# Attention values with the value matrix held in the array, two heads in column halves, and the exponentials scaled on ScalarE first

## What is computed

```python
def attend(q, k, v):
    s = jnp.einsum('bqhgd,bkhd->bhgqk', qblk, k) * scale
    p = jax.nn.softmax(s, axis=-1)
    return jnp.einsum('bhgqk,bkhe->bqhge', p, v)
...
    o1 = attend(dq[:, :, :, 0, None, :], dk[:, :, :, 0, :], dv)
    o2 = attend(dq[:, :, :, 1, None, :], dk[:, :, :, 1, :], dv)
    od = (o1 - lam * o2)[:, :, :, 0, :]
    od = rmsnorm(od, subln_g) * (1.0 - lambda_init)
    og = attend(gq.reshape(B, S, GQA_KV_HEADS, GQA_GROUP, HEAD_DIM), gk, gv)
    o = jnp.concatenate([od.reshape(B, S, DIFF_WIDTH), og.reshape(B, S, GQA_WIDTH)], axis=-1)
    return o @ w_out
```

## Time and profile before

| | |
|---|---|
| Time, median of 3 runs | 1468.42 us (1465.95 to 1468.68) |
| Profiled execution, its own time | 1464.05 us |
| Its span | 1462.2 us |
| Mean granted TensorE clock | 0.968 of full speed |
| Busy: PE, DVE, ACT, POOL | 1323.5, 1109.0, 630.1, 317.5 us |
| The 16 units | from 128.96 us (first exponential) to about 205 us |

### The profile page before, as it was taken

The page is one execution under the profiler, slowest core; times in us unless marked ns, Lnnn a source line. Parts: engine busy times, 40 slices in busy tenths (PEclk is TensorE's granted clock), DMA queues, the critical chain, the costliest instruction groups (busy, mean ns, idle before and its releaser), DMA issues.

```text
span 1462.2 us, 16524 instructions
## 1 busy us (share of the span) xinstructions
PE 1323.5 (91%) x5512; PEld 874.0 (60%) x5512; DVE 1109.0 (76%) x2315; ACT 630.1 (43%) x1322; POOL 317.5 (22%) x307
## 2 busy tenths in 40 slices
PE   9998899998797978697887799999999999999998
PEld 3876664543353424253343346678888877788887
DVE  6688857876776776766667777869998577799974
ACT  5343733222221222222221225567776445677752
POOL 0000003544344444344434430000110000011100
PEclk9999999999898989899898899999999999999999
DMA  9624457999999999999999996434545434345540
GB/s 392 271 116 190 162 248 317 419 422 421 421 422 420 421 422 421 421 414 421 414 421 407 414 416 265 171 117 157 189 173 196 156 118 167 115 178 198 201 144 30
DMA packets 50437, 416.32 MB, mean 285 GB/s; under 512 B 5552, under 2 KB 5680, under 8 KB 7088
## 3 DMA queue, kind: packets, MB, share of 16 engines
q0 software_dynamic: 36864, 268.45, 44.4%
q1 hardware_dynamic: 13488, 146.82, 26.3%
HBM read 414.20 MB, written 1.05 MB: 284 GB/s over the span
## 4 chain that ended last, share of the span: by engine, by line
PE 39%; DVE 36%; DMA 13%; issue 6%; ACT 3%; POOL 2%; DVEq 0%; SPq 0%; POOLq 0%; ACTq 0%
PE ps L1199 9%; DVE arena_r L592 8%; DMA ring<-in_uv,ids 6%; DMA arena<-in_uv,ids 6%; PE ps L1278 4%; PE ps L1280 4%; PE ps L1279 4%; DVE arena L2519 4%; DVE ring L2237 4%; DVE arena L2237 2%; DVE arena L2511 2%; DVE arena L2521 2%; PE ps L1172 2%; PE ps L1018 2%; PE ps L907 2%
## 5 line engine op out<-in xcount | busy, mean ns | idle before, releaser
L1199 PE MATMUL ps<-ring,arena 128*128 128x512 f32 x632 | 294.3, 616 | 51.5 <-ACT arena L1714 51.5
L2237 DVE CUSTOM_DVE_ANT_0 ring<-ring,arena 128x1024 f32<-128x1024 f32 x158 | 190.6, 1225 | 85.9 <-DMA ring<-in_uv,ids 85.5
L1199 PEld LDWEIGHTS ps<-ring,arena 128*128 128x128 f32 x632 | 122.3, 197 | 213.5 <-issue 143.6
L1486 PE MATMUL ps<-hpair,arena_r 128*128 128x512 f32 x704 | 244.3, 394 | 0.0
L592 DVE TENSOR_TENSOR arena_r<-ring,arena_r 128x1024 fp32r<-128x1024 f32 x152 | 185.5, 1223 | 57.3 <-ACT arena_r L577 53.6
L1199 PE MATMUL ps<-arena 128*128 128x512 f32 x392 | 186.5, 622 | 46.5 <-ACT arena L1714 46.3
L793 POOL DMA_INDIRECT ring<-in_uv,ids x158 | 177.8, 1126 | 227.2 <-PE ps L1199 175.4
L1488 PE MATMUL ps<-hpair,arena_r 128*128 128x256 f32 x704 | 195.0, 277 | 0.0
L577 ACT ACTIVATE arena_r<-ring 128x1024 fp32r<-128x1024 f32 x152 | 158.8, 1053 | 59.0 <-PE ps L1280 58.1
L793 POOL DMA_INDIRECT arena<-in_uv,ids x98 | 104.3, 1064 | 352.2 <-issue 246.5
L1199 PEld LDWEIGHTS ps<-arena 128*128 128x128 f32 x392 | 76.9, 199 | 148.5 <-issue 92.0
(11 more groups left out here) (337 smaller groups left out, 2049.2 us busy)
## 6 DMA issues: line engine op xcount, KB each, us to landing
ring<-in_lw SPq DMA_DIRECT2D x39, 2048.0 KB, 7.8
ring<-in_b1w SPq DMA_DIRECT2D x14, 2048.0 KB, 8.8
ring<-in_b1w SPq DMA_DIRECT2D x9, 1024.0 KB, 16.7
ring<-in_lw SPq DMA_DIRECT2D x8, 1024.0 KB, 5.1
wqb<-in_wq SPq DMA_DIRECT2D x4, 1024.0 KB, 9.0
arena<-in_wq SPq DMA_DIRECT2D x3, 1024.0 KB, 13.4
ring<-in_uv,ids POOLq DMA_INDIRECT x158, 16.9
ring<-in_lw SPq DMA_DIRECT2D x2, 1088.0 KB, 10.2
```

Of the source, the lines that this page charges most:

```text
L1199: last = nc.tensor.matmul(ps[:, 4 + 2 * c + b, :], diag[:, k % 4, :], vrows[place(n, k)][:, b * 512:(b + 1) * 512], start=False, stop=(clo ...
L1486: nc.tensor.matmul(ps[:, bank, :].rearrange("p (t n) -> p t n", t=2), high_of(l, p)[:, cols_], hpair[:, :, k, :], start=(k == 0), stop=Fal ...
L2237: V.tensor_tensor_reduce(out=urows[at], in0=urows[at], in1=hrow[:, c, :], scale=1.0, scalar=0.0, op0=ALU.mult, op1=ALU.add, accum_out=dots ...
```

## The change

Units of the grouped kind are done the other way round. The values of one key/value head (128 keys by 64 columns) become the weights and the transposed probabilities (128 keys by 128 queries) the moving side. The result comes out transposed: head dimension on partitions 0 to 63 for the first head, 64 to 127 for the second, 128 queries in the free dimension. The two heads so use two column halves of the array, and the loop over key chunks is now the outer one. This result is what `out_sums` needs as weights, so it is copied straight into the grouped half of `orow` (`grouped_rows`) and used from there: `turned` and `heads_in` for the grouped blocks go away, for both chunks.

Since queries are no longer on partitions, the reciprocals of the sums can't be applied on the way out. A new step, `act_scale`, scales the two exponentials of a grouped unit in place on ACT, before they are transposed; it waits for the reciprocals of DVE (`rz_ready`), and PE's `turn` waits for it (`scaled`). On ACT the order within a turn of the loop becomes: exponentials of m, `act_pt(m - 1)`, `act_rows(m - 2)`, `act_scale(m)`. `values(m)` waits until the rows of unit m - 1 are out of bank 6, where it was unit m - 2.

```diff
+        def of_kind(m):
+            kind = [(t < DIFF) for c, t in units()]
+            return sum(k == kind[m] for k in kind[:m + 1])
+        def grouped_rows(c):
+            return orow[:, c, 512:1024].rearrange("p (k n) -> p k n", k=4)
+        def act_scale(act, m):
+            act.wait_ge(rz_ready, of_kind(m))
+            for s in range(2):
+                last = nc.scalar.activation(E[:, m % 2, s, :], E[:, m % 2, s, :], ACT.Copy, scale=rz4[:, m % 4, s:s + 1])
+            last.then_inc(scaled, 1)
...
             else:
-                for s in range(2):
-                    last = nc.scalar.activation(orow[:, c, t * P + s * HD:t * P + (s + 1) * HD],
-                                                src[:, s * HD:(s + 1) * HD], ACT.Copy, scale=rz4[:, m % 4, s:s + 1])
+                last = nc.scalar.activation(grouped_rows(c)[:, t - DIFF, :], src, ACT.Copy)
...
-                pe.wait_ge(probs_ready, m + 1)
+                pe.wait_ge(probs_ready if t < DIFF else scaled, of_kind(m))
...
-                if m >= 2:
-                    pe.wait_ge(pv_out, m - 1)
+                if m >= 1:
+                    pe.wait_ge(pv_out, m)
...
-                    for s in range(2):
-                        for kc in range(4):
-                            last = nc.tensor.matmul(ps[:, 6, at + s * HD:at + (s + 1) * HD],
+                    for kc in range(4):
+                        for s in range(2):
+                            last = nc.tensor.matmul(ps[s * HD:(s + 1) * HD, 6, at:at + P],
+                                                    vrow[:, kc, 512 + s * HD:512 + (s + 1) * HD],
                                                     PT[:, m % 2, s, kc * P:(kc + 1) * P],
-                                                    vrow[:, kc, 512 + s * HD:512 + (s + 1) * HD],
-                                                    start=(kc == 0), stop=(kc == 3))
+                                                    start=(kc == 0), stop=(kc == 3), skip_group_check=True)
...
+                c = 1 if bank in (2, 3) else 0
                 for i in steps:
                     k = OUT_ORDER[i]
-                    last = nc.tensor.matmul(ps[:, bank, :], oT[:, k, :], out_weight(n, k), start=(i == 0),
+                    heads = oT[:, k, :] if k < DIFF else grouped_rows(c)[:, k - DIFF, :]
+                    last = nc.tensor.matmul(ps[:, bank, :], heads, out_weight(n, k), start=(i == 0),
...
                 if m == 10:
                     pe.wait_ge(pv_out, 8)
-                    pe.wait_ge(mod_out, MOD_A + 5)
-                    turned(0, range(4, KD), 7)
                 elif m == 11:
                     pe.wait_ge(rows_ready, 2)
-                    pe.wait_ge(o_out, 1)
+                    pe.wait_ge(mod_out, MOD_A + 5)
                     turned(0, range(4), 7)
...
-            turned(1, range(4, KD), 4)
             pe.wait_ge(exp_done, 32)
-            pe.wait_ge(o_out, 3)
             out_sums(0, 2, 0, 1)
...
+                if m >= 1:
+                    act_pt(act, m - 1)
                 if m >= 2:
                     act_rows(act, m - 2)
-                if m >= 1:
-                    act_pt(act, m - 1)
+                if t >= DIFF:
+                    act_scale(act, m)
...
-                elif m == 11:
-                    heads_in(1, range(4, KD), 7)
                 elif m == 12:
-                    heads_in(2, range(4), 7, con("subg"))
+                    heads_in(1, range(4), 7, con("subg"))
...
-            heads_in(3, range(4, KD), 4)
...
-                    dve.sem_inc(probs_ready, 1)
+                    dve.sem_inc(rz_ready, 1)
```

More of the change, by code:

```diff
@@ L359, in program @@
         pt_done, pt_act, pv_done, pv_out = (sem(n) for n in ("pt_done", "pt_act", "pv_done", "pv_out"))
+        rz_ready, scaled = sem("rz_ready"), sem("scaled")
         gd_ready, gb_done, gb_out = sem("gd_ready"), sem("gb_done"), sem("gb_out")
@@ L1041, in _ @@
                     pe.wait_ge(pv_out, 8)
-                    pe.wait_ge(mod_out, MOD_A + 5)
-                    turned(0, range(4, KD), 7)
                 elif m == 11:
                     pe.wait_ge(rows_ready, 2)
-                    pe.wait_ge(o_out, 1)
+                    pe.wait_ge(mod_out, MOD_A + 5)
                     turned(0, range(4), 7)
                 elif m == 12:
-                    pe.wait_ge(o_out, 2)
+                    pe.wait_ge(o_out, 1)
                     out_sums(0, 7, 0, 1)
@@ L1147, in _ @@
             cleared(4, 5)
-            pe.wait_ge(o_out, 4)
+            pe.wait_ge(o_out, 2)
             out_sums(0, 2, 4, 5, 6, 7)
@@ L1687, in _ @@
             rows_in(0, (0, 7))
-            heads_in(4, range(4), 0, con("subg"))
+            heads_in(2, range(4), 0, con("subg"))
             softmax(0, 0)
@@ L2073, in attn_probs @@
                         .then_inc(probs_ready, 1)
-                    dve.wait_ge(probs_ready, m + 1)
+                    dve.wait_ge(probs_ready, of_kind(m))
                 else:
-                    dve.sem_inc(probs_ready, 1)
+                    dve.sem_inc(rz_ready, 1)
             attn_max(0)
```

## The result

Seven executions of the changed kernel have a median of 1471.5 us (1470.1 to 1473.7), seven of the kernel before on the same chip 1466.6 us (1465.3 to 1468.7). The ratio is 1.0028 with a 95% interval of 1.0019 to 1.0038: some 4.1 us slower by the ratio, 4.9 us by the medians. The profiled execution took 1470.54 us (span 1468.7). The forecast of 1470.1 stood on a median before of 1468.4; measured side by side the kernel before is 1.8 us faster than that, so the forecast's own statement, 1.7 us slower, is too small by 2.4 to 3.2 us although its absolute time is near.

What follows compares the result with a forecast made beforehand. No engine alone bounds the units; PE's chain ends them and passes delay on unchanged. ACT's scales delay turn(11) by 3.0 us, shorter PE work leaves +1.7: 1468.4 + 1.7 = 1470.1 us, range 1465.5 to 1474.0.

Steps and rivals of the forecast that it cites:

- The likeliest case: Units 7 to 11: ACT is the longest and delays PE's end of the units, +1.7 us; chance 0.42.
- The rival on the other side: Units: scales hide in ACT's idle time, only PE's gain shows, -3 to -4.4 us, 1464.5; chance 0.12.
- The values: Grouped values on PE: 16 matmuls in column halves take 1.15 us with both mode changes, against 1.83 before.
- rival 1: Grouped values on PE: column halves don't overlap, values take 1.95 us, +4.0 us, 1472.4; chance 0.18.
- rival 3: Grouped values on PE: weight loads wait for matmuls, 2.6 to 3.4 us, +6 to +8, 1475; chance 0.04.
- The scales: ACT in grouped units: 0.73 us for each scale, 1.35 us a pair, eight pairs 10.8 us.
- The walk: Units 7 to 11 followed on ACT: turn(8) +1.4, turn(9) +1.45, turn(10) +1.8, turn(11) +3.0 us.
- the predicted +1.7: Unit 12's modulation total on PE starts at 186.9 against 185.17 us, passed unchanged to the kernel's end.
- I count nothing for chunk 0 up to unit 7: Units up to 7: lateness from the scales is taken in by DVE's longer chain and shorter values; no cost.
- From there to the end the same distance as before: After unit 12's modulation total: the remaining time to the kernel's end is unchanged.
- worth nothing: Second dropped turned, at 205.7 us: its 0.44 us of PE gain nothing, since PE then waits for the second norm.
- a rival of its own: Units 10 and 11: PE's new waits bring half clock, +3.7 to +6 us, about 1473; chance 0.13.

Runs made afterwards that it cites:

- e3: Changed kernel without the scales on ACT, grouped heads left unnormalised: 1464.5 us, ratio 0.9990 to the kernel before.
- e4: Kernel before with the scales on ACT put in and rows copied without a scale, old values kept: 1475.4 us, ratio 1.0064.
- e1: Changed kernel with matmuls on zeros filling PE's idle time before unit 5's turn and unit 11's scores: 1468.2 us, ratio 1.0012.
- e2: Changed kernel with two output products of chunk 1 moved ahead of the second norm's transposes: 1468.7 us, ratio 1.0018.
- e8: Changed kernel with output products moved into PE's waits, chunk 0's differential blocks turned later, zero matmuls in units 1 and 5: 1465.0 us, ratio 0.9995.
- e5: Changed kernel with both scales of a grouped unit on DVE behind its reciprocal instead of ACT: 1469.8 us, ratio 1.0026.
- e10: Changed kernel with DVE's reciprocals of seven grouped units (not unit 11) taken ahead of modulation pieces: 1465.8 us, ratio 0.9996.
- e6: Changed kernel with one head's scale on ACT and the other's on DVE: 1467.7 us, ratio 1.0012.
- e7: Changed kernel with the grouped values' loops swapped, one column half after the other: 1471.8 us, ratio 1.0045.
- e11: Changed kernel with scales split between ACT and DVE, work and fillers moved into PE's waits, and early reciprocals: 1466.1 us, ratio 1.0003.

## Why the prediction was right, and where its sizes were off

**The sign and the mechanism.** The likeliest case was that ACT becomes the longest from unit 7 on and pushes the end of the units back. The trace shows it step by step, and e3 and e4 bear out that the scales are the price (9.4 us on the old values). The rival on the other side would have decided itself at `turn(8)` at 163.5 or before; it came at 165.43.

**The values.** 1.15 us taken, 1.09 measured (1.03 from start to the next `scores`); rival 1 would have had 1.95. It falls, and so does rival 3: even in sequence, where two neighbours never share a half, 16 instructions took 1.58 us and not 2.6 to 3.4. The rule of the Trainium skill, page "TensorE: Matmul & The Clock Gate", section The mechanism, that a weight load overlaps running matmuls only if its row group differs, is not borne out as it stands: both halves use all rows, and their 16 loads (0.85 us of PEld) and 16 matmuls fit in 1.03 us. The same section also lets a load run ahead into a background weight buffer; that would fit, and no run here tests it.

**The scales.** 0.73 each and 1.35 a pair taken, 0.72 and 1.33 measured.

**The walk.** Taken against measured: `turn(8)` +1.4 and +1.9, `turn(9)` +1.45 and +2.1, `turn(10)` +1.8 and +2.3, `turn(11)` +3.0 and +3.3, the total 186.9 and 187.56, which is +2.55 against the predicted +1.7 (the prediction counts from the chain's 185.17; there it is 187.63 and +2.46). Two terms of it were mis-sized. The first is "I count nothing for chunk 0 up to unit 7": `turn(4)` was 0.7 us ahead, then the wait of 1.79 us in unit 5 came with half clock, and `turn` and the differential values behind it took 3.56 us from 152.23 to 155.79 where they need less (1.9 at full clock: 0.93 and 0.98 from row to row in unit 3 of e1). That 1.6 us put unit 6's `turn` 1.06 late, and it is all there at `turn(8)`: from `turn(4)` to it the changed kernel needs 17.7 us, e1, e2 and e8 at full clock 16.1, the kernel before 15.1. So at full clock this execution would have had `turn(8)` near +0.3 (0.7 ahead, 1.0 longer), not at the +1.4 of the walk. That the measured +1.9 lies near +1.4 is luck: the walk had too much for ACT there and nothing for the clock. The second is unit 11: its `turn` ran at half clock, 1.76 for 1.09, which is 0.67 of the piece from `turn(11)` to the total (5.97 us instead of the predicted 5.55, and 5.30 at full clock in e1). Between the two the walk was right: `turn(8)` to `turn(11)` was to grow by 1.6 us and grew by 1.4 at full clock.

**The end of the kernel.** "From there to the end the same distance as before" failed, in one place. Up to the second norm's transposes it held: 24.53 us from the total, 24.48 before. Then the first query took 4.42 us instead of 2.80, 1.62 more at half clock. The step of the prediction is its account of the dropped `turned(1, range(4, KD), 4)` as "worth nothing". Its 0.44 us were worth nothing as time, which is what it said; but with it gone PE stood idle for 1.81 us ahead of those transposes, where it had 0.73 and 0.41 with work between them. +2.55 and +1.62 are 4.2 us; 4.0 are left at the piece near 249.5, 4.9 between the medians, 4.1 by the ratio. The wait alone doesn't decide it: e1, e5 and e10 had the same 1.8 us of idle and kept full clock, e3, e6 and e7 lost it.

**The clock.** It was named as a rival of its own (+3.7 to +6, about 1473), for units 10 and 11, one of the three places where it fell. In the profiled executions the three falls cost 1.6 us (unit 5), 0.67 (unit 11) and 1.5 (first query, from its start to the work behind it), some 3.8 of the 4.0 us of lateness at 250 us. Without them the units would have lost some 0.25 us up to the total instead of the predicted 1.7: the new wait on ACT and DVE still costs 2.4 us up to `turn(11)` (1.0, 0.4 and 0.9 from `turn(4)` on), and the shorter PE work gives back 1.4 behind it and 0.7 ahead of `turn(4)`. So the forecast was right on the sign and near in size, its chain of waits is the one in the trace, and the size came out near because falls of the clock that it did not count stood in for a lateness at unit 8 that it had too high. This is from single executions. Over all executions the mean granted clock is 0.966 for the changed kernel and 0.968 for the kernel before and for e1, so with the fillers the mean clock is that of before, and e1 is still 0.12% slower (0.02 to 0.22%). The 2.56 us wait in unit 1 was followed by a fall in all three executions that had it (e1, e2, e4); the waits in unit 5, in unit 11 and ahead of the first query were in some and not in others, so their price is a mean over executions; e1 and e2 bound it loosely (2.3 and 1.5 us better by ratio, with overlapping intervals).

**What the prediction did not see.** It took ACT's 1.35 us as what can't be hidden, and carried DVE's reciprocal as a given time. e10 moved only the reciprocals and took back 4.7 us by ratio, the whole loss, with the pairs of scales still on ACT and a fall of the clock still in unit 11. So the queue in front of a reciprocal that had become urgent is a cause, and the 1.33 us on ACT are affordable without it. It is not shown to be the largest: e8, with full clock from `turn(4)` to the total, work in the waits and the late reciprocals, took back as much (0.33%), and e6, with one scale on DVE, gained more than e10 up to the total in the trace. Removing it also shortens the wait in unit 5 from 1.79 to 0.54 us, where the clock then held. At equal clock the order is worth 2.7 us up to `turn(10)`; how the rest of the 4.7 divides is not separated.

**Open.** What e10 or e11 would give with unit 11's reciprocal moved too, which no run did; which of the waits is followed by the lower clock in a given execution, and whether a lead of 1 to 3 us at the expert stage is worth anything at the end.

## What to carry to other kernels

Trading work between engines moves more than busy time: before you price a new step, ask which signal it hangs on, and find what stands ahead of that signal in its engine's queue, since a result that was allowed to be late before (here a reciprocal) becomes urgent with a new reader. If a change shortens PE's work in a ring that PE does not bound, the saved time turns into idle time, and idle time may cost clock; price a dropped filler by the gap it leaves, not by its length. Compare a change with its parts alone: here the good part was worth 1.5 us and the bad one cost 9.4, and what the two lost together came back either by another order on an engine that the change had left alone or by work put into the waits. When single profiles are compared, look for falls of the clock first: two kernels that pass a landmark at the same time may do so for different reasons, as e7 and the changed kernel do.

## What the runs showed of the hardware

- With 64 columns of weights for each head and 128 columns moving, two heads in column halves of the array: 16 float32 matmul instructions take 1.02 us from their start to the next work when the halves alternate, and 1.51 us when one half's eight instructions follow the other's; the old form with 128 columns of weights and 64 moving took 1.73.
- A granted clock of 0.50 (matmuls up to twice as long) came behind PE idle times of 1.05 (e6, unit 10), 1.79 (changed, unit 5), 1.92 (e10, unit 11), 2.25 (changed, unit 11) and 2.56 us (unit 1 of e1, e2 and e4), and not behind 3.23 us in e5, whose next `turn` took 1.09 us, nor behind 2.09 us in e11. Behind 1.81 us in unit 5 of e2 the clock stayed full, with the same instructions up to there as in the changed kernel. The first query took 4.42 or 4.43 us in the changed kernel, e3, e6 and e7 and 2.80 in e1, e5 and e10, with 1.80 or 1.81 us of idle ahead in all seven. The length of the gap alone does not tell.
- DVE scales 128x512 float32 values in place by a value for each partition in 0.88 us a pair, ACT in 1.33 us.
